# The inverse of the gated delta rule as stacked 64x64 blocks, two 64x64 tiles of the array for each product

## The chip, the cores and the metric

The kernel runs on one core of one Trainium2 chip. The metric is the time of one execution on the device, in microseconds (us); smaller is better.

## What is computed

One layer of a hybrid decoder block: 512 tokens, width 1024. A combined projection feeds sliding-window attention and a gated delta rule; their outputs are mixed, and a product-key mixture of experts (PEER) follows. The change lies in the delta rule alone: 8 heads, keys and values of 128, chunks of 64 tokens. Cut to what matters:

```python
a_low = where(strict, einsum('bhncd,bhnsd->bhncs', k_beta, kc) * decay, 0)   # 64x64 for each head and chunk
t_mat = triangular_solve(eye + a_low, eye)                                   # the inverse, 64x64
u = einsum('bhncs,bhnse->bhnce', t_mat, v_beta)
w = einsum('bhncs,bhnsd->bhncd', t_mat, k_beta * exp(gc))
qk = einsum('bhncd,bhnsd->bhncs', qc, kc) * decay
# then, one chunk after the other: v_new, o and the state
```

All of it is fp32.

## The kernel before

The program is written out phase by phase, with a queue of instructions for each engine and semaphores set by hand. The phase of the change, `phase_delta`, goes over four tiles of 128 tokens (`NT`), each of which holds two chunks of 64. Its tensors are `[128 partitions, 8 heads, 128]`; the work goes in two halves of four heads (`G = 4`, `q` = 0 or 1), one PSUM bank for each half.

In the inverse the two 64x64 matrices of a head's two chunks stand as the diagonal blocks of one 128x128 matrix, the other two blocks being zero. In a tile the order is: sums and transposes (L1019 to L1028), spreads of coefficients (L1034), the product KK of keys (L1050, banks 2 and 3), which VectorE multiplies by the masked decay `AT` that GpSimd has made (L985), and the product QK (L1058). Then come six levels of block doubling.

- Level 0: TensorE transposes AT (L1071, "P"), VectorE masks the result into `prod` (L1250) and makes `inv` and `invT` (L1291, L1292).
- Levels 1 to 5: P is the product of AT and inv (L1073, banks 0 and 1); VectorE masks it into `prod`; Q is the product of invT and prod (L1085, levels 1 to 4 alone, banks 2 and 3) and of prod and invT (L1086, banks 6 and 7); VectorE subtracts them from inv (L1298) and invT (L1300).

After the levels, u and w (L1092, L1093) use invT with 128x128 operands, and the chunk-by-chunk part follows (L1105 to L1121). TensorE takes its work in program order: P of half 0, P of half 1, Q of half 0, Q of half 1. P of a half waits for that half's invT of the level before (semaphore `D`), Q for that half's prod (`Pm`), and VectorE for `P` and `Q`.

Between these, `fill(n)` puts n passes of an independent projection (L1002, 512 columns, fp32r): 16 of them after P of level 0, and 3 after P of levels 1, 2 and 3, the last tile having none in levels 1 to 3. The number of fill passes in the phase is fixed. An fp32 product is two passes on TensorE, each with a weight load and a matmul record; a transpose is one.

Of the kernel before, what the change touches and what calls it, by code (L numbers as in the profile page):

```python
# [13 lines left out]
P = 128  # L14
KB = 1024
SEQ = 512
D = 1024
# [902 lines left out]
def phase_delta(nc, m, a, st, first_slabs):  # L920
# [6 lines left out]
    invT, q1, prod = m.at("invT", full, 72), m.at("q1", full, 76), m.at("prod", full, 76)  # L927
    AT, u = m.at("AT", full, 80), m.at("u", full, 80)
    inv, wT = m.at("inv", full, 84), m.at("wT", full, 84)
# [23 lines left out]
    with nc.Block() as block:  # L953
# [22 lines left out]
        @block.gpsimd  # L976
        def _(pool):
            nc.gpsimd.memset(S[:], 0.0).then_inc(z["prep0"], 1)
            for t in range(NT):
                if t:  # L980
                    pool.wait_ge(z["o"], t)
                for h in range(2):
                    hs = slice(G * h, G * h + G)
                    pool.wait_ge(z["E"], t * 2 + (h + 1))
                    nc.gpsimd.tensor_tensor(AT[:, hs, :], E[:, hs, :],  # L985
                                            m.strict[:].rearrange("p (o n) -> p o n", o=1).to_broadcast([P, G, P]),
                                            ALU.mult).then_inc(z["Es"], 1)

        @block.tensor
        def _(pe):  # L990
# [17 lines left out]
            def tile(t):  # L1008
# [53 lines left out]
                for l in range(6):  # L1062
                    for q in range(2):
                        if l == 0:
                            pe.wait_ge(z["AT"], t * 2 + (q + 1))
                        else:
                            pe.wait_ge(z["D"], t * 12 + (2 * l + q - 1))
                        for h in range(G * q, G * q + G):
                            o = bank[q][:, P * (h % G):P * (h % G) + P]
                            if l == 0:  # L1070
                                last = pe.transpose(o, AT[:, h, :], m.ident[:])  # L1071
                            else:
                                last = pe.matmul(o, AT[:, h, :], inv[:, h, :], start=True, stop=True)  # L1073
                        last.then_inc(z["P"], 1)
# [5 lines left out]
                    for q in range(2):  # L1080
                        pe.wait_ge(z["Pm"], t * 12 + (2 * l + q + 1))
                        for h in range(G * q, G * q + G):
                            cols = slice(P * (h % G), P * (h % G) + P)
# [12 lines left out]
                for c in range(2):  # L1096
                    rows = slice(CHUNK * c, CHUNK * c + CHUNK)
                    if c == 0:
                        pe.wait_ge(z["uwe"], t + 1)
                        if first:  # L1100
                            pe.wait_ge(z["prep0"], 1)
# [22 lines left out]
            pe.wait_ge(z["prep"], 1)  # L1124
# [75 lines left out]
        def _(dve):  # L1200
# [8 lines left out]
            v.tensor_scalar(sel[:], m.same[:], last2[:, 0:1], None, ALU.mult).then_inc(z["prep"], 1)  # L1209

            for t in range(NT):
# [35 lines left out]

                def by(q, dst, src, b, done):
# [19 lines left out]
                for q in range(2):  # L1268
                    dve.wait_ge(z["KK"], t * 2 + (q + 1))
                    dve.wait_ge(z["Es"], t * 2 + (q + 1))  # L1270
                    by(q, AT, AT[:, G * q:G * q + G, :], 2, z["AT"])
# [4 lines left out]
                eye = m.ident[:].rearrange("p (o n) -> p o n", o=1).to_broadcast([P, G, P])  # L1276
                dve.wait_ge(z["AT"], t * 2 + 2)
                for q in range(2):
                    hs = slice(G * q, G * q + G)
                    ins = v.tensor_tensor(invT[:, hs, :], AT[:, hs, :], m.above[:].rearrange("p (o n) -> p o n", o=1)  # L1280
                                          .to_broadcast([P, G, P]), ALU.mult)
                own(dve, c, ins)
                for l in range(6):
                    for q in range(2):
                        dve.wait_ge(z["P"], t * 12 + (2 * l + q + 1))
                        by(q, prod, m.level[:, l:l + 1, :].to_broadcast([P, G, P]), 0, z["Pm"])
                    if l == 0:
                        dve.wait_ge(z["Pm"], t * 12 + 2)
                        for q in range(2):
                            hs = slice(G * q, G * q + G)  # L1290
                            v.tensor_tensor(inv[:, hs, :], eye, prod[:, hs, :], ALU.subtract)  # L1291
                            v.tensor_tensor(invT[:, hs, :], eye, invT[:, hs, :], ALU.subtract).then_inc(z["D"], 1)  # L1292
# [963 lines left out]
```

## Time and profile before

| | |
|---|---|
| time, median of 3 runs | 2443.43 us (2440.55 to 2449.08) |
| span of the profiled execution | 2444.4 us |
| the delta phase in it | about 411 to 787 us |
| levels 1 to 5 of the inverse, four tiles | 119.70 us |
| TensorE busy, whole span | 2299.5 us (94%) |
| VectorE busy, whole span | 1774.4 us (73%) |

The profiled execution's own span is 1.0 us over the median of the runs, so the sum can be made against either. A level's time is read from one start of L1073 to the next. A matmul record lasts longer than the spacing to the next one, because passes overlap in the array: what a pass costs is the spacing, (length of a merged row − length of one record) / (passes − 1).

### The profile page before, as it was taken

What the parts mean: (1) busy time and instruction counts of PE and PEld (TensorE: products, weight loads), DVE (VectorE), ACT (ScalarE), POOL (GpSimd) and SP (SyncE); (2) the same over time, 40 slices, a digit from 0 to 9 for tenths busy, and PEclk for the clock granted to TensorE, in tenths of its full rate; (3) what the DMA queues carried; (4) which work ended last, traced back from release to release, by engine and by line L of the source; (5) the groups of instructions that cost most, each with busy time, mean ns of one, the idle gap of its engine ahead of it and who ended that gap; (6) DMA issues with size and microseconds to landing.
All of it is one profiled execution on the core that took longest, in us unless ns stands there. A gap on an engine that the chain in (4) does not pass through costs nothing.

```text
span 2444.4 us, 33257 instructions
## 1 busy us (share of the span) xinstructions
PE 2299.5 (94%) x12845; PEld 1989.1 (81%) x12845; DVE 1774.4 (73%) x3248; ACT 935.5 (38%) x1601; POOL 723.1 (30%) x637
## 2 busy tenths in 40 slices
PE   7898897899999999898999999899999999999998
PEld 2686776888888787678989999888888888888887
DVE  4488885554655764418978999778888888878787
ACT  2235776031131332325555555433333333333332
POOL 0444672000000000005656433533333333333330
PEclk9999997999999999899999999999999999999999
DMA  8332331010011323214333466998998889899883
GB/s 276 108 100 92 115 104 35 27 35 19 26 40 63 115 86 121 69 52 149 128 122 131 158 199 194 338 350 317 323 319 310 320 324 318 308 328 349 316 313 136
DMA packets 224989, 442.21 MB, mean 181 GB/s; under 512 B 22423, under 2 KB 138304, under 8 KB 224576
## 3 DMA queue, kind: packets, MB, share of 16 engines
q1 hardware_dynamic: 177040, 270.19, 33.0%
q0 software_dynamic: 45568, 163.60, 18.6%
q10 hardware_dynamic: 2224, 6.29, 0.6%
q8 instruction: 102, 1.67, 0.3%
q14 instruction: 55, 0.45, 0.1%
HBM read 394.16 MB, written 45.88 MB: 180 GB/s over the span
## 4 chain that ended last, share of the span: by engine, by line
PE 45%; DVE 8%; ACT 2%; issue 1%; POOL 0%; ACTq 0%; DVEq 0%
PE bank L1929 22%; PE bank L1827 5%; DVE hot_j L2145 5%; PE bank L1915 4%; PE bank L1913 4%; PE bank L1914 4%; PE bank L1833 3%; PE bank L1797 2%; DVE hot_i L2140 2%; ACT ha L1977 1%; PE bank L1807 1%; PE bank L1849 1%; DVE o_nat L2209 0%; DVE o_nat L2208 0%; PE bank L1897 0%
## 5 line engine op out<-in xcount | busy, mean ns | idle before, releaser
L1759 POOL TENSOR_TENSOR ua_lo<-ua,ua_hi 128x512 fp32r<-128x512 f32 x128 | 204.2, 1601 | 456.6 <-ACT ua L1964 456.4
L1929 PE MATMUL bank<-vt_hi,wg_hi 128*128 128x512 f32 x768 | 247.8, 404 | 5.0 <-DVE wg_lo L2199 4.8
L1752 POOL DMA_INDIRECT ug<-in_peer_u_dram,gidx x128 | 145.1, 1133 | 327.5 <-DVE ug L2155 324.5
L1929 PE MATMUL bank<-vt_lo,wg_hi 128*128 128x512 f32 x768 | 238.6, 392 | 0.0
L1929 PE MATMUL bank<-vt_hi,wg_lo 128*128 128x512 f32 x768 | 237.9, 391 | 0.0
L2181 DVE TENSOR_TENSOR vt_lo<-vt_raw,vt_hi 128x1024 fp32r<-128x1024 f32 x128 | 156.5, 1223 | 92.5 <-ACT vt_hi L2051 92.5
L1781 POOL DMA_INDIRECT vg<-in_peer_v_dram,gidx x128 | 131.5, 1027 | 238.9 <-DVE g_acc L2170 226.8
L1827 PE MATMUL bank<-h_hi,ua_hi 128*128 128x384 f32 x512 | 184.2, 360 | 12.3 <-ACT ha L1977 12.0
L1913 PE MATMUL bank<-h_hi,uT_hi 128*128 128x384 f32 x512 | 176.8, 345 | 0.0
L1827 PE MATMUL bank<-h_lo,ua_hi 128*128 128x384 f32 x512 | 173.8, 339 | 0.0
L2051 ACT ACTIVATE vt_hi<-vt_raw 128x1024 fp32r<-128x1024 f32 x128 | 135.2, 1056 | 98.7 <-PE bank L1929 98.7
L2062 ACT ACTIVATE wg_hi<-wt 128x384 fp32r<-128x384 f32 x128 | 67.3, 526 | 274.6 <-DVE wt L2194 271.4
L1915 PE MATMUL bank<-h_hi,uT_lo 128*128 128x384 f32 x512 | 171.8, 335 | 0.0
L1929 PEld LDWEIGHTS bank<-vt_hi,wg_hi 128*128 128x128 f32 x768 | 135.1, 189 | 44.9 <-issue 24.1
L1914 PE MATMUL bank<-h_lo,uT_hi 128*128 128x384 f32 x512 | 171.2, 334 | 0.0
L1929 PEld LDWEIGHTS bank<-vt_hi,wg_lo 128*128 128x128 f32 x768 | 144.5, 188 | 31.8
L1929 PEld LDWEIGHTS bank<-vt_lo,wg_hi 128*128 128x128 f32 x768 | 144.4, 188 | 31.6
L2170 DVE SCALAR_TENSOR_TENSOR g_acc<-vg,g_hw,g_acc 128x1024 f32<-128x1024 f32 x127 | 162.9, 1282 | 2.4 <-DMA vg<-in_peer_v_dram,gidx 1.3
L2155 DVE SCALAR_TENSOR_TENSOR ug<-ug,h2n 128x1024 f32<-128x1024 f32 x128 | 156.1, 1221 | 1.0 <-DMA ug<-in_peer_u_dram,gidx 0.9
L1953 ACT ACTIVATE uT_hi<-bank 128x512 fp32r<-128x512 f32 x128 | 76.0, 594 | 190.1 <-PE bank L1797 187.1
L2150 DVE TENSOR_TENSOR uT_lo<-bank,uT_hi 128x512 fp32r<-128x512 f32 x128 | 88.3, 690 | 81.9 <-ACT uT_hi L1953 81.9
L2145 DVE TENSOR_SCALAR hot_j<-iota,picked,picked 128x128 f32<-128x128 f32 x384 | 145.9, 444 | 0.0
(433 smaller groups left out, 5707.2 us busy)
## 6 DMA issues: line engine op xcount, KB each, us to landing
u_raw<-in_peer_u_dram SPq DMA_DIRECT2D x128, 512.0 KB
vt_raw<-in_peer_v_dram SPq DMA_DIRECT2D x128, 512.0 KB
gates<-g_stage SPq DMA_DIRECT2D x12, 2048.0 KB, 9.0
gate<-gates SPq DMA_DIRECT2D x32, 768.0 KB, 7.6
pj_raw<-in_w_in_dram SPq DMA_DIRECT2D x16, 1024.0 KB, 5.2
ada_w<-in_w_ada_dram POOLq DMA_DIRECT2D x32, 512.0 KB, 4.6
hid_keep<-ha POOLq DMA_DIRECT2D x64, 192.0 KB
hl<-hid_keep SPq DMA_DIRECT2D x64, 192.0 KB
```

The costliest lines, as they stand in the source:

```text
L1752: nc.gpsimd.indirect_dma_start(ug[s % RING][:], None, u_rows, bass.IndirectOffsetOnAxis(m.gidx[:, s:s + 1].bitcast(U32), 0)).then_inc(s_ug ...
L1759: nc.gpsimd.tensor_tensor(ua_lo[b % 2][:, 4 * q:4 * q + 4, :], ua[b % 2][:, 4 * q:4 * q + 4, :], ua_hi[b % 2][:, 4 * q:4 * q + 4, :].bitca ...
L1827: last = pe.matmul(o, ua_hi[b % 2][:, k, :], (m.h2_lo if low else m.h2_hi)[:, k, P:], start=(n == 0), stop=False)
L1913: pe.matmul(o, uT_hi[f % 2][:, k, :], m.h2_hi[:, k, P:], start=(k == 0), stop=False)
L1914: pe.matmul(o, uT_hi[f % 2][:, k, :], m.h2_lo[:, k, P:], start=False, stop=False)
L1915: last = pe.matmul(o, uT_lo[f % 2][:, k, :], m.h2_hi[:, k, P:], start=False, stop=(k == KC - 1))
L1929: ins = pe.matmul(y_bank[t][q][:], w[n % 2][:, tok], v[n % 2][:, 512 * q:512 * q + 512], start=(first and i == 0), stop=(last and i == 2))
L2051: nc.scalar.activation(v_hi[n % 2][:], v_raw[n % 4][:], ACT.Copy).then_inc(x["vhi"], 1)
L2145: ins = v.tensor_scalar(B[n % 4][:, t, :], m.iota[:], jT[:, col], gT[:, col], ALU.is_equal, ALU.mult)
L2155: v.scalar_tensor_tensor(ug[s % RING][:], ug[s % RING][:], 1.0, m.h2n[:], ALU.mult, ALU.mult, accum_out=h_raw[:, s:s + 1]).then_inc(x["dot ...
L2170: ins = v.scalar_tensor_tensor(acc[:], vg[s % RING][:], h_w[:, s:s + 1], acc[:], ALU.mult, ALU.add)
L2181: v.tensor_tensor(v_lo[n % 2][:], v_raw[n % 4][:], v_hi[n % 2][:].bitcast(F32), ALU.subtract)\
```

## The change

The two 64x64 blocks of a head are no longer kept as a 128x128 matrix with two zero blocks, but stacked: chunk 0 on partitions 0 to 63, chunk 1 on partitions 64 to 127, 64 columns a head. Each 128x128 product of the inverse becomes two 64x64 products, `for rows in CH`: one reads partitions 0 to 63 and writes partitions 0 to 63 of the bank, the other reads 64 to 127 and writes 64 to 127. VectorE's operations over the inverse have 256 elements a partition in place of 512. The first level's transposes become products with a stacked identity `eye`. The last level writes the result back into the two diagonal blocks of the 128x128 `invT`, whose other blocks were zeroed once. KK is computed for the two diagonal blocks alone, and GpSimd masks them with two operations of 64 partitions. The core of the diff:

```diff
+    pair = [P, DNH, CHUNK]
+    prod, AT = m.at("prod", pair, 76), m.at("AT", pair, 80)
+    inv, tinv = m.at("inv", pair, 84), m.at("tinv", pair, 86)
+    eye, near = m.at("eye", [P, CHUNK], 96), m.at("near", [P, CHUNK], 96.25)
+    step = m.at("step", [P, 6, CHUNK], 96.5)
+    CH = [slice(CHUNK * c, CHUNK * c + CHUNK) for c in range(2)]
...
+            nc.gpsimd.memset(invT[:], 0.0).then_inc(z["prep0"], 1)
+            pool.wait_ge(z["prep0"], 2)
...
-                    nc.gpsimd.tensor_tensor(AT[:, hs, :], E[:, hs, :],
-                                            m.strict[:].rearrange("p (o n) -> p o n", o=1).to_broadcast([P, G, P]),
-                                            ALU.mult).then_inc(z["Es"], 1)
+                    if t * 2 + h:
+                        pool.wait_ge(z["Es"], t * 4 + 2 * h)
+                    for c, rows in enumerate(CH):
+                        if c:
+                            pool.wait_ge(z["Es"], t * 4 + 2 * h + 1)
+                        nc.gpsimd.tensor_tensor(AT[rows, hs, :], E[rows, hs, rows],
+                                                m.strict[rows, rows].rearrange("p (o n) -> p o n", o=1)
+                                                .to_broadcast([CHUNK, G, CHUNK]), ALU.mult).then_inc(z["Es"], 1)
...
-                    last = pe.matmul(bank[2 + h // G][:, P * (h % G):P * (h % G) + P], kT[:, h, :], kb[:, h, :],
-                                     start=True, stop=True)
+                    cols = slice(CHUNK * (h % G), CHUNK * (h % G) + CHUNK)
+                    for rows in CH:
+                        last = pe.matmul(bank[2 + h // G][rows, cols], kT[:, h, rows], kb[:, h, rows],
+                                         start=True, stop=True)
...
-                            o = bank[q][:, P * (h % G):P * (h % G) + P]
-                            if l == 0:
-                                last = pe.transpose(o, AT[:, h, :], m.ident[:])
-                            else:
-                                last = pe.matmul(o, AT[:, h, :], inv[:, h, :], start=True, stop=True)
+                            cols = slice(CHUNK * (h % G), CHUNK * (h % G) + CHUNK)
+                            for rows in CH:
+                                last = pe.matmul(bank[q][rows, cols], AT[rows, h, :],
+                                                 inv[rows, h, :] if l else eye[rows, :], start=True, stop=True)
...
                             if l < 5:
-                                pe.matmul(bank[2 + q][:, cols], invT[:, h, :], prod[:, h, :], start=True, stop=True)
-                            last = pe.matmul(bank[6 + q][:, cols], prod[:, h, :], invT[:, h, :], start=True, stop=True)
+                                for rows in CH:
+                                    pe.matmul(bank[2 + q][rows, cols], tinv[rows, h, :], prod[rows, h, :],
+                                              start=True, stop=True)
+                            for rows in CH:
+                                last = pe.matmul(bank[6 + q][rows, cols], prod[rows, h, :], tinv[rows, h, :],
+                                                 start=True, stop=True)
...
+            v.tensor_tensor(eye[:], m.ident[:, CH[0]], m.ident[:, CH[1]], ALU.add).then_inc(z["prep"], 1)
+            v.tensor_tensor(near[:], m.above[:, CH[0]], m.above[:, CH[1]], ALU.add)
+            own(dve, c, v.tensor_tensor(step[:], m.level[:, :, CH[0]], m.level[:, :, CH[1]], ALU.add))
...
+                def stacked(b):
+                    return bank[b][:, 0:G * CHUNK].rearrange("p (h n) -> p h n", h=G)
...
-                            v.tensor_tensor(inv[:, hs, :], inv[:, hs, :],
-                                            bank[2 + q][:].rearrange("p (h n) -> p h n", h=G), ALU.subtract)
-                        v.tensor_tensor(invT[:, hs, :], invT[:, hs, :],
-                                        bank[6 + q][:].rearrange("p (h n) -> p h n", h=G), ALU.subtract)\
-                            .then_inc(z["D"], 1)
+                            v.tensor_tensor(inv[:, hs, :], inv[:, hs, :], stacked(2 + q), ALU.subtract)
+                            ins = v.tensor_tensor(tinv[:, hs, :], tinv[:, hs, :], stacked(6 + q), ALU.subtract)
+                        else:
+                            dve.wait_ge(z["prep0"], 2)
+                            for rows in CH:
+                                ins = v.tensor_tensor(invT[rows, hs, rows], tinv[rows, hs, :],
+                                                      bank[6 + q][rows, 0:G * CHUNK].rearrange("p (h n) -> p h n", h=G),
+                                                      ALU.subtract)
+                        ins.then_inc(z["D"], 1)
```

## Rows read from the trace of the kernel before

**Rows 1.** The page: engines over the span, and the granted clock in 40 slices
```profile
PE 2299.5 (94%) x12845; PEld 1989.1 (81%) x12845; DVE 1774.4 (73%) x3248; ACT 935.5 (38%) x1601; POOL 723.1 (30%) x637
...
PEclk9999997999999999899999999999999999999999
```

**Rows 2.** Windows: levels 1 to 5 of tiles 0 to 3
```profile
core 0: us, PE busy (x) PEld busy (x) DVE busy (x) ACT busy (x) POOL busy (x), PEclk, DMA share, GB/s
458.80:489.36 30.56, 28.62 (x234) 27.23 (x234) 18.55 (x29) 0.00 (x0) 0.00 (x0) 1.00 0.01 1
550.48:580.73 30.25, 28.31 (x235) 27.07 (x233) 17.91 (x28) 0.00 (x0) 0.00 (x0) 1.00 0.00 1
643.01:673.59 30.58, 28.64 (x234) 27.23 (x234) 18.55 (x29) 0.00 (x0) 0.00 (x0) 1.00 0.00 1
734.67:762.98 28.31, 26.37 (x225) 25.45 (x224) 17.95 (x28) 0.84 (x1) 0.00 (x0) 1.00 0.03 10
```

**Rows 3.** Timeline of TensorE, level 3 of the last tile (no fill)
```profile
start us, us, engine line op out<-in xcount [idle before <-releaser]
...
752.40 1.06 PE L1073 MATMUL bank<-inv,AT 128*128 128x128 f32 x8
753.94 1.16 PE L1073 MATMUL bank<-inv,AT 128*128 128x128 f32 x8 [0.48 <-DVE invT L1300]
754.93 0.39 PE L1085 MATMUL bank<-prod,invT 128*128 128x128 f32 x2
...
758.51 0.28 PE L1073 MATMUL bank<-inv,AT 128*128 128x128 f32 x1
```

**Rows 4.** Timeline of TensorE, level 2 of tile 1 (with fill)
```profile
556.53 1.06 PE L1073 MATMUL bank<-inv,AT 128*128 128x128 f32 x8
...
559.30 0.40 PE L1002 MATMUL bank<-h_hi,fl_hi 128*128 128x512 f32 x1
559.53 0.40 PE L1002 MATMUL bank<-h_lo,fl_hi 128*128 128x512 f32 x1
...
563.34 0.39 PE L1073 MATMUL bank<-inv,AT 128*128 128x128 f32 x2
```

**Rows 5.** Timeline of TensorE: attention, 64-column and 64-row operands in turn
```profile
248.10 1.15 PE L638 MATMUL bank<-pT,av 128*64 128x128 f32 x16
249.17 1.14 PE L608 MATMUL bank<-kn,aq 64*128 64x256 f32 x8
```

**Rows 6.** Timeline of TensorE: delta phase, 64-column operands on one side alone
```profile
768.88 1.96 PE L1105 MATMUL bank<-states,wT 128*64 128x128 f32 x16 [0.31 <-ACT wT L1188]
770.76 2.00 PE L1110 MATMUL bank<-qg,states 128*128 128x64 f32 x16
...
773.59 0.39 PE L1002 MATMUL bank<-h_lo,fl_hi 128*128 128x512 f32 x1
773.82 0.40 PE L1002 MATMUL bank<-h_hi,fl_lo 128*128 128x512 f32 x1
774.14 1.04 PE L1115 MATMUL bank<-vnew,kdec 64*128 64x128 f32 x7
```

**Rows 7.** Groups by form: VectorE's 512- and 256-element operations
```profile
L1250 DVE TENSOR_TENSOR prod<-level,bank 128x512 f32<-128x512 f32 x48 | 32.6, 685 | 13.4 <-PE bank L1073 13.1
L798 DVE SCALAR_TENSOR_TENSOR sc<-bank,qrs,amask 128x256 f32<-128x256 f32 x64 | 26.4, 475 | 0.2 <-PE bank L608 0.2
L819 DVE COPY aq<-bank 128x256 f32<-128x256 f32 x16 | 6.4, 403 | 0.0
```

**Rows 8.** Groups by form: GpSimd's products
```profile
L985 POOL TENSOR_TENSOR AT<-E,strict 128x512 f32<-128x512 f32 x8 | 13.8, 1730 | 303.8 <-DVE E L1264 303.8
L528 POOL TENSOR_TENSOR ada_w<-ada_w 128x256 f32<-128x256 f32 x32 | 31.6, 988 | 2.5
```

**Rows 9.** Timelines of TensorE and VectorE: level 0, last tile and tile 2
```profile
727.61 0.66 PE L1071 MATMUL bank<-ident,AT 128*128 128x128 f32 x4 [2.67 <-DVE AT L1250]
728.93 1.01 PE L1071 MATMUL bank<-ident,AT 128*128 128x128 f32 x4 [0.67 <-DVE AT L1250]
...
731.01 0.63 PE L1002 MATMUL bank<-h_hi,fl_hi 128*128 128x512 f32 x1
731.44 0.63 PE L1002 MATMUL bank<-h_lo,fl_hi 128*128 128x512 f32 x1
...
643.01 0.68 PE L1073 MATMUL bank<-inv,AT 128*128 128x128 f32 x4 [0.81 <-DVE invT L1292]
```

More of the change, by code:

```diff
@@ L926, in phase_delta @@
     E = m.at("E", full, 68)
-    invT, q1, prod = m.at("invT", full, 72), m.at("q1", full, 76), m.at("prod", full, 76)
-    AT, u = m.at("AT", full, 80), m.at("u", full, 80)
-    inv, wT = m.at("inv", full, 84), m.at("wT", full, 84)
+    pair = [P, DNH, CHUNK]
+    invT, q1 = m.at("invT", full, 72), m.at("q1", full, 76)
+    prod, AT = m.at("prod", pair, 76), m.at("AT", pair, 80)
+    inv, tinv = m.at("inv", pair, 84), m.at("tinv", pair, 86)
+    u, wT = m.at("u", full, 80), m.at("wT", full, 84)
+    eye, near = m.at("eye", [P, CHUNK], 96), m.at("near", [P, CHUNK], 96.25)
+    step = m.at("step", [P, 6, CHUNK], 96.5)
+    CH = [slice(CHUNK * c, CHUNK * c + CHUNK) for c in range(2)]
     sq = m.at("dn_sq", [P, 2 * DNH, P], 76)
@@ L1082, in tile @@
                         for h in range(G * q, G * q + G):
-                            cols = slice(P * (h % G), P * (h % G) + P)
+                            cols = slice(CHUNK * (h % G), CHUNK * (h % G) + CHUNK)
                             if l < 5:
-                                pe.matmul(bank[2 + q][:, cols], invT[:, h, :], prod[:, h, :], start=True, stop=True)
-                            last = pe.matmul(bank[6 + q][:, cols], prod[:, h, :], invT[:, h, :], start=True, stop=True)
+                                for rows in CH:
[4 more added lines that the diff above has]
+                                                 start=True, stop=True)
                         last.then_inc(z["Q"], 1)
@@ L1100, in tile @@
                         if first:
-                            pe.wait_ge(z["prep0"], 1)
+                            pe.wait_ge(z["prep0"], 2)
                     else:
@@ L1123, in tile @@
                 last.then_inc(z["o"], 1)
-            pe.wait_ge(z["prep"], 1)
+            pe.wait_ge(z["prep"], 2)
             for t in range(NT):
@@ L1269, in _ @@
                     dve.wait_ge(z["KK"], t * 2 + (q + 1))
-                    dve.wait_ge(z["Es"], t * 2 + (q + 1))
-                    by(q, AT, AT[:, G * q:G * q + G, :], 2, z["AT"])
+                    dve.wait_ge(z["Es"], t * 4 + 2 * q + 2)
+                    hs = slice(G * q, G * q + G)
+                    v.tensor_tensor(AT[:, hs, :], AT[:, hs, :], stacked(2 + q), ALU.mult).then_inc(z["AT"], 1)
                 for q in range(2):
@@ L1275, in _ @@
                     by(q, E, E[:, G * q:G * q + G, :], 6, z["QKT"])
-                eye = m.ident[:].rearrange("p (o n) -> p o n", o=1).to_broadcast([P, G, P])
+                unit = eye[:].rearrange("p (o n) -> p o n", o=1).to_broadcast([P, G, CHUNK])
                 dve.wait_ge(z["AT"], t * 2 + 2)
@@ L1279, in _ @@
                     hs = slice(G * q, G * q + G)
-                    ins = v.tensor_tensor(invT[:, hs, :], AT[:, hs, :], m.above[:].rearrange("p (o n) -> p o n", o=1)
-                                          .to_broadcast([P, G, P]), ALU.mult)
+                    ins = v.tensor_tensor(tinv[:, hs, :], AT[:, hs, :], near[:].rearrange("p (o n) -> p o n", o=1)
+                                          .to_broadcast([P, G, CHUNK]), ALU.mult)
                 own(dve, c, ins)
@@ L1285, in _ @@
                         dve.wait_ge(z["P"], t * 12 + (2 * l + q + 1))
-                        by(q, prod, m.level[:, l:l + 1, :].to_broadcast([P, G, P]), 0, z["Pm"])
+                        v.tensor_tensor(prod[:, G * q:G * q + G, :], step[:, l:l + 1, :].to_broadcast([P, G, CHUNK]),
+                                        stacked(q), ALU.mult).then_inc(z["Pm"], 1)
                     if l == 0:
@@ L1290, in _ @@
                             hs = slice(G * q, G * q + G)
-                            v.tensor_tensor(inv[:, hs, :], eye, prod[:, hs, :], ALU.subtract)
-                            v.tensor_tensor(invT[:, hs, :], eye, invT[:, hs, :], ALU.subtract).then_inc(z["D"], 1)
+                            v.tensor_tensor(inv[:, hs, :], unit, prod[:, hs, :], ALU.subtract)
+                            v.tensor_tensor(tinv[:, hs, :], unit, tinv[:, hs, :], ALU.subtract).then_inc(z["D"], 1)
                         continue
```

## The prediction

> **What bounds the kernel now.** I read the page first: TensorE is busy 94% of the span and VectorE 73%, and the granted clock is full nearly everywhere [rows 1]. That is an average over phases, so I cut out the stretches the change touches: levels 1 to 5 of the four tiles last 30.56, 30.25, 30.58 and 28.31 us, together 119.70 us or 4.9% of the span, with TensorE busy 93% of each at full clock and VectorE about 60% [rows 2]. Nothing outside the delta phase is touched, and the phases follow each other, so what the inverse saves comes off the end nearly whole.
>
> Then one level. In the last tile, which has no fill there, P of one level starts at 752.40 and P of the next at 758.51, so a level is 6.11 us [rows 3]. It is 48 passes: 8 + 8 for P, 16 + 16 for Q. The first row gives a pass: (1.06 − 0.28) / 7 = 0.112 us, so 48 × 0.112 = 5.38 us. The rest, 0.73 us, is mainly the wait of the second half's P for VectorE's invT (0.48). With three fill passes of 0.23 us a level is 6.81 us, 556.53 to 563.34 [rows 4]. So TensorE's stream of passes sets the level, and VectorE's six operations of 0.685 us [rows 7] mostly hide under it.
>
> **The price of a 64x64 pass.** A head's product is two fp32 passes now and four small ones afterwards, so the change pays if a small pass costs under half of 0.112 us. No row shows a pass with 64 rows, 64 weight columns and 64 moving columns. The nearest:
>
> - Halving one side alone gives nothing: 64 weight columns with 128 moving ones cost (1.96 − 0.28) / 15 = 0.112 us, 128 weight columns with 64 moving ones (2.00 − 0.28) / 15 = 0.115 [rows 6]. The longer of the two sides sets the pace. With both at 64 a single stream should come to half, about 0.055.
> - Two tiles at once give another half. In attention, L638 uses 64 weight columns and changes between the two column halves: 16 passes in 1.15 us, (1.15 − 0.27) / 15 = 0.059 each, where L1105 with the same shape in one half pays 0.112. L608 changes between the two row halves: (1.14 − 0.38) / 7 = 0.109 for 256 moving columns, where 128 cost 0.112 in one stream [rows 5, 6].
>
> Both together make a quarter of 0.112, or 0.028, and half of 0.059, or 0.030. I take 0.030. Ends: 0.0275 below, and above a full 0.112 (nothing gained from either).
>
> The Trainium skill ("TensorE: Matmul & The Clock Gate", "Back-to-back issue gap") has a rule against the change: with hardware decode off the sequencer spends about 62 ns on a matmul, and small ones go no faster. L638's 0.059 lies just under it, but in a burst of 16 alone, so the trace barely speaks against it. By 62 ns a level's 96 passes would be 5.95 us, and by 0.030 they are 2.88.
>
> **Levels, part by part.** VectorE: 512 elements take 0.685 us and start 0.60 apart; 256 fewer elements, at the rate that 0.403 to 0.475 us for 256 from PSUM confirms [rows 7], make about 0.42 us, 0.34 apart. Six of them are 2.1 us a level, still under TensorE.
>
> A changed level without fill:
> - 96 passes × 0.030 = 2.88 us;
> - a wait: after the last pass of Q has started, it lands (0.22), VectorE does inv and tinv (0.34 + 0.42) and the signals take 0.09: 1.07 us, of which P of the first half covers 16 × 0.030 = 0.48. That leaves 0.57.
>
> Sum 3.45 us for 6.11. With fill there come 3 × 0.23 = 0.69, and two changes between full and small tiles. At such a change the gap is wider: L1105's last start, 768.88 + 1.96 − 0.28 = 770.56, to 770.76 is 0.20 for 0.11 and the row's first pass adds 0.05; 773.82 to 774.14 is 0.32 for 0.23 and the first pass adds 0.1 [rows 6]. So 0.14 to 0.19 each, and I take 0.16. Sum 4.46 us for 6.81. Level 1 begins with both halves ready and so costs 4.2 and 3.2. Level 5 has only 64 passes (1.92), the wait, and a tail of two operations of 64 partitions in place of one, 3.1 us in all.
>
> Per tile with fill: 4.2 + 4.46 + 4.46 + 3.45 + 3.1 = 19.7 us; last tile: 3.2 + 3 × 3.45 + 3.1 = 16.7. Against [rows 2]: (30.56 + 30.25 + 30.58) − 3 × 19.7 = 32.3, and 28.31 − 16.7 = 11.6. **Levels: −43.9 us.**
>
> **Level 0 and KK.** The eight transposes (one pass each) become 32 small passes, 0.96 us for 0.9, plus changes of tile size on both sides of them and before level 1. The 16 fill passes stay. Where TensorE comes late (the last tile) this costs 0.1 us a tile. Where it waits for VectorE, 0.85 us in tile 0 and 0.81 in tile 2 [rows 9], VectorE's shorter operations end the wait, which gives 0.7 each. Together **−1.2 us**. KK (16 passes to 32 small ones) gains up to 0.8 us on TensorE, which I cost at nothing: behind it TensorE waits 2.67 us for AT anyway [rows 9]. If that cover were gone it would be a gain.
>
> GpSimd's two masks per half: 128x512 took 1.73 us in the mean, a 256-element product elsewhere 0.99 [rows 8]. Two in a row are 1.3 (half price) to 3.5 us (full price), and I take 2.0. AT is then up to 0.3 us later, which VectorE's shorter AT operation (−0.26) pays back. At full price 4 × 1.7 = 7 us would be lost; behind the second mask in its queue is nothing but the next tile's. The memset, `eye`, `near` and `step` lie under ACT's squares at the phase's start: nothing, at most 1 us. No DMA changes.
>
> **The clock.** In level 0 of the last tile the fill passes stand 0.43 apart instead of 0.23 (731.01, 731.44) [rows 9]: half clock, after 2.67 us of waiting. The shorter KK lengthens that wait, and the levels leave the array emptier. One more such stretch in a tile, 8 slow passes × 0.2, costs 1.6 us. I put in **+3 us** for four tiles (between 0 and 6.4).
>
> **Sum:** 2443.4 − 43.9 − 1.2 + 3 = 2401.3; I say **2402 us**, −1.7%.
>
> **Rivals.**
> 1. *Two tiles do not run at once.* L638's two halves share a bank but read all rows; L608's two row halves write two banks. The changed products read different rows and write one bank, which no row shows. If they take turns, a pass costs 0.0545: 5.23 us a level, with the wait about 5.4 (fill 6.4), level 5 3.9; per tile 28.4 and 25.3. Saved: 91.4 − 85.2 + 28.3 − 25.3 = 9 us, so 2436 us (2434 to 2441 with clock and level 0). For it: nothing in the rows. The Trainium skill says it outright ("TensorEngine Tiling (Array Packing)", "Gotcha 1: PSUM Pressure"): different row tiles cannot use one PSUM bank simultaneously. No run here shows it.
> 2. *The stream of instructions is the bound.* Each small pass still has its weight load and its matmul, so a level has 192 instructions for 96. If no pass goes below L638's 0.059, a level is 5.7 (fill 6.7) and the time is 2440 to 2444 us: no change. The skill's 62 ns would give the same.
> 3. *The clock falls in the levels.* Passes at 0.055 and fill at 0.43: 2441 us; half of the stretch so, 2421. Against it: full clock in all of [rows 2], whose waits are under 0.5 us.
> 4. *Slower.* The array drains at every change of tile, which happens after every two passes. Then a pair pays part of the 0.16 us, and 0.055 + 0.04 a pass makes 9.1 us a level. Level time goes over today's once a pass passes about 0.060. At 0.095 the loss is 3 us × 16 levels + 4 × 2 = 56 us: 2500 us. At the bound of 0.112 it is about 100 us. L638 and L608, which change tile every four passes, speak against it.
> 5. *The pace is good but something else takes part back* (VectorE as the bound, GpSimd's masks at full price, late fill): passes of 0.04 or 10 us lost elsewhere, 2414.
>
> **Chances.** Forecast (2393 to 2408) 0.60, rival 5 0.15, rival 1 0.10, rival 2 0.05, rival 3 0.04, rival 4 0.06. What a measurement tells from no change is 0.3%, 7.3 us: faster is under 2436. Faster: 0.60 + 0.15, half of rival 1 (0.05) and of rival 3 (0.02), 0.82; within it: the rest of rivals 1, 2 and 3, 0.12; slower 0.06. Range 2390 to 2434: forecast, rival 5 and a part of 1 and 3; its upper end stands for passes of 0.054. The forecast's own is 2393 (0.0275 and no clock loss) to 2408.
>
> **What would show it.** In the timeline P starts of L1073's successor 3.4 to 3.5 us apart in the last tile and 4.4 to 4.6 with fill; 16 passes of P in 0.7 us; the windows of levels 1 to 5 at about 76 us in sum; clock 1.00 in them; VectorE's operations 0.42 us; GpSimd's masks 0.8 to 1.1. A merged row of 16 passes that lasts 1.1 us means rival 1 or 2: starts in pairs tell 1 from 2. It would be wrong if small passes stand 0.055 or more apart.

## The result, and the profile after

Over four executions each the changed kernel takes 2410.61 us (2405.57 to 2412.26) and the kernel before 2445.63 us (2440.55 to 2449.08): ratio 0.9848, interval 0.9830 to 0.9867. The forecast was 2402 us, so the sign is right and 35 of the 41 us came. The profiled execution of the changed kernel has a span of 2410.4 us for 2444.4. One execution among all the runs below, 3206.55 us at a granted clock of 0.65 throughout, is in no median.

The windows of levels 1 to 5, tiles 0 to 3, in the changed kernel (against [rows 2]; columns as there), and below them the whole delta phase:

```profile
core 0: us, PE busy (x) PEld busy (x) DVE busy (x) ACT busy (x) POOL busy (x), PEclk, DMA share, GB/s
461.79:481.08 19.29, 18.01 (x459) 15.53 (x458) 10.73 (x29) 0.00 (x0) 0.00 (x0) 1.00 0.01 3
544.23:563.54 19.31, 18.03 (x459) 15.53 (x458) 10.74 (x29) 0.00 (x0) 0.00 (x0) 1.00 0.02 4
626.63:645.93 19.30, 18.02 (x459) 15.53 (x458) 10.74 (x29) 0.00 (x0) 0.00 (x0) 1.00 0.04 12
708.86:725.31 16.45, 15.12 (x449) 13.92 (x448) 10.73 (x29) 0.75 (x1) 0.00 (x0) 1.00 0.05 19
412.62:749.72 337.10, 313.74 (x3506) 278.23 (x3507) 160.10 (x417) 79.42 (x154) 15.42 (x16) 0.91 0.13 37
```

The four levels' windows sum to 74.35 us for 119.70, at full clock and with twice the records. The last row is the news: the whole phase has a mean granted clock of 0.91. (The window ends just after the last tile's product o has begun; that product takes 2.05 us in both kernels.) The same window of the kernel before reads 0.95:

```profile
411.60:785.90 374.30, 348.40 (x2450) 318.73 (x2451) 197.01 (x409) 79.32 (x154) 13.84 (x8) 0.95 0.11 33
```

So the phase went from 374.30 to 337.10 us, 37.2 less, where the levels alone gave 45.35. Laid out by stage (from the first matmul of each to that of the next, sum of four tiles, us; fill counts to the stage that it follows; gcn and cf are the two sets of coefficients that the spreads copy over the columns; states and o are the chunk-by-chunk part):

| stage | before | after | difference |
|---|---|---|---|
| squares, transposes | 34.72 | 36.93 | +2.2 |
| spreads of gcn | 32.31 | 33.42 | +1.1 |
| spreads of cf | 21.49 | 21.80 | +0.3 |
| KK | 9.94 | 7.80 | -2.1 |
| QK and the wait for AT | 15.70 | 16.32 | +0.6 |
| level 0 | 27.08 | 31.37 | **+4.3** |
| levels 1 to 5 | 119.70 | 74.35 | **-45.35** |
| u and w | 23.81 | 24.20 | +0.4 |
| states | 67.25 | 68.64 | +1.4 |
| o | 22.29 | 22.27 | 0 |

One level with fill, in TensorE's timeline of the changed kernel (tile 1, against [rows 4]):

```profile
start us, us, engine line op out<-in xcount [idle before <-releaser]
...
548.20 0.68 PE L1085 MATMUL bank<-inv,AT 64*64 64x64 f32 x16
549.13 0.68 PE L1085 MATMUL bank<-inv,AT 64*64 64x64 f32 x16 [0.25 <-DVE tinv L1324]
...
550.33 0.40 PE L1014 MATMUL bank<-h_lo,fl_hi 128*128 128x512 f32 x1
550.65 0.33 PE L1099 MATMUL bank<-prod,tinv 64*64 64x64 f32 x4
550.82 0.28 PE L1102 MATMUL bank<-tinv,prod 64*64 64x64 f32 x4
550.93 0.28 PE L1099 MATMUL bank<-prod,tinv 64*64 64x64 f32 x4
...
552.65 0.56 PE L1085 MATMUL bank<-inv,AT 64*64 64x64 f32 x11
```

P starts at 548.20 and again at 552.65, 4.45 us. Sixteen passes of P last 0.68, so (0.68 - 0.22) / 15 = 0.031 us each; from the second on, Q's groups of four start 0.117 apart (550.82, 550.93), 0.029 a pass. The wait for `tinv` is 0.25. From 550.33 to 550.65, fill to small tile, is 0.32 for 0.23. In the last tile P starts at 715.47 and 718.87, 3.40 us.

And level 0 of the last tile (against [rows 9]):

```profile
701.40 0.68 PE L1085 MATMUL bank<-eye,AT 64*64 64x64 f32 x16 [2.53 <-DVE AT L1295]
702.97 1.12 PE L1085 MATMUL bank<-eye,AT 64*64 64x64 f32 x16 [0.89 <-DVE AT L1295]
...
704.62 0.63 PE L1014 MATMUL bank<-h_lo,fl_hi 128*128 128x512 f32 x1
705.04 0.63 PE L1014 MATMUL bank<-h_hi,fl_lo 128*128 128x512 f32 x1
```

A wait of 2.53 us, one of 0.89, and then fill passes start 0.43 apart (704.62, 705.04), the clock's lower level of 1.2 GHz, until from 706.28 on they are back at 0.23. The changed kernel has this in every tile, after waits for AT of 1.96, 1.97, 1.97 and 2.53 us; in tile 0 the slow passes go from 455.74 to 460.17, ten gaps. The record of the granted clock has 61 us at the lower level within the phase, and 41 before.

In the kernel before the waits were 1.72, 1.75, 1.75 and 2.67 us, and the clock fell in tile 1 and the last alone. Tiles 1 and 2 had the same waits; the length of the second row (1.09 for 0.66) shows the clock:

```profile
543.38 0.66 PE L1071 MATMUL bank<-ident,AT 128*128 128x128 f32 x4 [1.75 <-DVE AT L1250]
544.71 1.09 PE L1071 MATMUL bank<-ident,AT 128*128 128x128 f32 x4 [0.66 <-DVE AT L1250]
...
636.55 0.66 PE L1071 MATMUL bank<-ident,AT 128*128 128x128 f32 x4 [1.75 <-DVE AT L1250]
637.87 0.66 PE L1071 MATMUL bank<-ident,AT 128*128 128x128 f32 x4 [0.67 <-DVE AT L1250]
```

So the length of the wait alone does not decide. What ends the two waits is seen in VectorE's timeline of tile 0, changed kernel:

```profile
451.52 1.21 DVE L1223 TENSOR_TENSOR fl_lo<-fl_raw,fl_hi 128x1024 fp32r<-128x1024 f32 x1
452.65 0.41 DVE L1295 TENSOR_TENSOR AT<-AT,bank 128x256 f32<-128x256 f32 x1
454.21 0.42 DVE L1295 TENSOR_TENSOR AT<-AT,bank 128x256 f32<-128x256 f32 x1 [1.15 <-POOL AT L997]
```

The first half's AT comes when VectorE gets to it in its own queue, the second half's when GpSimd has done its masks (L997).

The rest of the kernel took 3.2 us more (1.0 ahead of the phase, 2.2 behind it), where no instruction differs. Profiles differ by as much: among the thirteen of this study the phase begins between 405.6 and 413.5 us, and what follows it takes 1656.6 us in the kernel before and 1657.4 to 1661.2 in the others. Whether the 2.2 us behind it are chance is not shown.

### The profile page after: what moved, and what is told of

It reads as the page before. It is cut to its first block, busy times and chain, and to the rows that moved or that the text cites. A ratio compares the mean times of both kernels' runs of the same rounds, so it can differ in the third digit from the quotient of the medians.

```text
span 2410.4 us, 35403 instructions
## 1 busy us (share of the span) xinstructions
PE 2266.5 (94%) x13901; PEld 1949.0 (81%) x13901; DVE 1738.7 (72%) x3259; ACT 935.9 (39%) x1601; POOL 721.0 (30%) x646
## 4 chain that ended last, share of the span: by engine, by line
PE 45%; DVE 8%; ACT 2%; issue 1%; DMA 0%; POOL 0%; ACTq 0%; DVEq 0%; POOLq 0%
PE bank L1958 22%; PE bank L1856 5%; DVE hot_j L2174 5%; PE bank L1944 4%; PE bank L1942 4%; PE bank L1943 4%; PE bank L1862 3%; PE bank L1826 2%; DVE hot_i L2169 2%; PE bank L1836 1%; ACT ha L2006 1%; PE bank L1878 1%; DMA vg<-in_peer_v_dram,gidx 0%; DVE o_nat L2238 0%; DVE o_nat L2237 0%
## 5 line engine op out<-in xcount | busy, mean ns | idle before, releaser
L1781 POOL DMA_INDIRECT ug<-in_peer_u_dram,gidx x128 | 144.3, 1127 | 330.4 <-DVE ug L2184 327.3
```

The costliest lines, as they stand in the source:

```text
L1781: nc.gpsimd.indirect_dma_start(ug[s % RING][:], None, u_rows, bass.IndirectOffsetOnAxis(m.gidx[:, s:s + 1].bitcast(U32), 0)).then_inc(s_ug ...
```

## The experiments

The questions: what makes the levels short (theory A: two tiles at once, not the smaller shape), how much of it needs VectorE's shorter operations, and where the 8 us between the levels' gain and the phase's went (theory C: the clock, lowered by the wait for AT). There are eleven runs, of which one is the changed kernel again and one repeats another run. Where no interval is given the time is that of a single execution, and the reading rests on its profile. In the code, "..." stands for the rest of a line, or for lines between.

### Both products on one tile

```diff
-                            for rows in CH:
+                            for rows in ((CH[0], CH[0], CH[1]) if l else CH):
                                 last = pe.matmul(bank[q][rows, cols], AT[rows, h, :], ...
```

In levels 1 to 5 chunk 0's products are computed twice on their own tile, and chunk 1's once. Q has the same edit.

> In levels 1 to 5 the product of chunk 0 is computed twice, both times on tile rows 0-63 / columns 0-63; the product of chunk 1 once. A level has 144 small passes in place of 96, 96 of them on one tile. Theory A (a tile takes 0.055 us a pass and the two tiles run at once): the tile with 96 passes sets the level, 96 x 0.0545 = 5.2 us and a wait, so a level without fill is 5.4 to 5.8 us in place of 3.40, and a half's P of 24 passes lasts about 0.95 us from first to last start. Theory B (all passes go through one point that takes 0.029 us each): 144 x 0.029 = 4.2 us and a wait, so a level of 4.5 to 4.8 us and 0.67 us for a half's P.

Time 2450.32 us. The window of levels 1 to 5 in the last tile (it was 16.45 us), and the start of level 1's Q in TensorE's timeline:

```profile
736.06:762.97 26.91, 26.89 (x673) 26.49 (x672) 11.06 (x28) 0.73 (x1) 0.00 (x0) 1.00 0.04 13
```
```profile
737.97 0.39 PE L1099 MATMUL bank<-prod,tinv 64*64 64x64 f32 x6
738.21 0.39 PE L1102 MATMUL bank<-tinv,prod 64*64 64x64 f32 x6
```

Six passes, four on tile 0 and two on tile 1, every 0.233 us: that is 4 x 0.058, tile 0's passes one after the other, with tile 1's hidden beside them. The change has four passes there, in 0.117: half as many passes again double the price. A level without fill is 5.74 us (P from 741.71 to 747.44), inside theory A's range and not B's 4.5 to 4.8. A 64x64 pass costs 0.058 on its tile, and only the second tile makes 0.029 of it. The levels sum to 116.93 us, nearly the 119.70 of before.

### A third tile beside the two

```diff
+                            if l:
+                                pe.matmul(bank[2 + q][CH[1], over], AT[CH[0], h, :], inv[CH[0], h, :], start=True, stop=True)
                             for rows in CH:
                                 last = pe.matmul(bank[q][rows, cols], AT[rows, h, :], ...
```

The same number of extra products, but on the tile that reads rows 0 to 63 and writes partitions 64 to 127 (Q alike); their results are not used.

> As many passes as in the kernel with chunk 0 doubled (144 a level), but the extra product runs on a third tile (rows 0-63, columns 64-127) and its result goes to a part of a bank that nobody reads. Theory A (tiles are independent, issue is fast): the third tile costs nothing, level without fill 3.4 to 3.6 us. Theory B (one point, 0.029 us a pass): 4.5 to 4.8 us, the same as with the extra product on the same tile.

Time 2414.8 us. TensorE's timeline in P of the last tile: L1086 is the extra product, L1088 the two of the change:

```profile
714.75 0.22 PE L1088 MATMUL bank<-inv,AT 64*64 64x64 f32 x2
714.76 0.22 PE L1086 MATMUL bank<-inv,AT 64*64 64x64 f32 x1
714.80 0.22 PE L1088 MATMUL bank<-inv,AT 64*64 64x64 f32 x2
```

Three passes now start in the 0.05 to 0.06 us in which two did. The levels sum to 79.08 us for 74.35: 50% more passes for 6% more time. Most of that 6% is in one row of the groups, levels 1 to 5 of tile 1:

```profile
L1088 PE MATMUL bank<-inv,AT 64*64 64x64 f32 x160 | 6.7, 224 | 0.9 <-issue 0.9
```

0.9 of the 1.1 us by which this tile is longer is idle time that no wait explains, in the middle of a row: in its last level 16 passes of P have started by 560.1, and the 17th starts at 561.21. So the supply of instructions (rival 2) may begin to show at three tiles; at the two of the change it is the single tile's 0.058 that binds.

### Chunk 0 first, then chunk 1

```diff
-                        for h in range(G * q, G * q + G):
-                            for rows in CH:
+                        for rows in CH:
+                            for h in range(G * q, G * q + G):
```

The same products in another order within a half: 8 passes of P, or 16 of Q, on one tile before the other's.

> The same products in another order: in each half first all of chunk 0 (one tile), then all of chunk 1 (the other tile), so the tile changes every 8 or 16 passes and not every 2. If the array starts a tile's pass as soon as that tile is free, looking at least 8 to 16 passes ahead: level unchanged, 3.4 to 3.6 us without fill. If it looks ahead only a few passes, the two tiles run one after the other: 0.055 a pass, a half's P of 16 passes 0.85 us and a level of 5.4 to 5.8 us.

Time 2442.99 us, nearly that of the kernel before. The levels sum to 100.64 us, 19 under those of before, but level 0 takes 35.33 and 68 us of the phase are at the lower clock. TensorE's timeline where Q's last half meets the next level's P (L1099, L1101: Q of chunk 1; L1085: P of chunk 0):

```profile
740.54 0.28 PE L1099 MATMUL bank<-prod,tinv 64*64 64x64 f32 x2
...
740.77 0.22 PE L1099 MATMUL bank<-prod,tinv 64*64 64x64 f32 x1
740.78 0.27 PE L1085 MATMUL bank<-inv,AT 64*64 64x64 f32 x1
...
740.95 0.22 PE L1085 MATMUL bank<-inv,AT 64*64 64x64 f32 x1
740.95 0.22 PE L1101 MATMUL bank<-tinv,prod 64*64 64x64 f32 x1
741.00 0.74 PE L1085 MATMUL bank<-inv,AT 64*64 64x64 f32 x13
```

Up to 740.77 the four passes from 740.54 on, all on one tile, take 0.23: 0.058 each. At the change of tile the next tile's passes begin while the last four of the old one (740.77 to 740.95) are still starting: pairs for 0.23 us, then single file again. So TensorE looks only a few passes ahead, which is what the rows allow; what limits it inside, no run tells. The order `for h: for rows` of the change is what earns 26.3 (100.64 - 74.35) of the levels' 45 us.

### The tile changed every four passes

```diff
                         for h in range(G * q, G * q + G):
-                            if l < 5:
-                                for rows in CH:
-                                    pe.matmul(bank[2 + q][rows, cols], tinv[rows, h, :], ...
-                            for rows in CH:
-                                last = pe.matmul(bank[6 + q][rows, cols], prod[rows, h, :], ...
+                            for rows in CH:
+                                if l < 5:
+                                    pe.matmul(bank[2 + q][rows, cols], tinv[rows, h, :], ...
+                                last = pe.matmul(bank[6 + q][rows, cols], prod[rows, h, :], ...
```

P takes the heads in twos, in the same way.

> The same products, but the tile changes after four passes and not after two (P takes two heads of chunk 0, then two of chunk 1; Q both products of a head's chunk 0, then both of chunk 1). The run with chunk 0's products all first had 16 passes of P in 0.96 us for 0.68, so a change of tile hid about 0.1 us, two passes of 0.055. Theory J (each change hides about that much, which is all of two passes and half of four, in both directions): passes at 0.028 to 0.035 still, a level without fill 3.4 to 3.8 us, levels 1 to 5 of the four tiles 74 to 80 us. Rival K (only neighbours that belong to different tiles overlap, one pair for each change): passes at 0.042 or more, a level of 4.3 us or more, 90 us or more in sum.

Time 2415.72 us; the levels sum to 75.54 us, 1.2 more than the change has. In TensorE's timeline of the last tile a level is 721.69 - 718.25 = 3.44 us:

```profile
718.25 0.73 PE L1086 MATMUL bank<-inv,AT 64*64 64x64 f32 x16
...
721.69 0.73 PE L1086 MATMUL bank<-inv,AT 64*64 64x64 f32 x16
```

Theory J holds: four passes on one tile, then four on the other, still pair almost fully. The look-ahead spans four passes and not eight (P of the run before has eight on a tile, and its half took 0.96 us for 0.68).

### VectorE's operations doubled

```diff
+                        if l:
+                            v.tensor_tensor(spare[q][:], step[:, l:l + 1, :].to_broadcast([P, G, CHUNK]), stacked(q), ALU.mult)
                         v.tensor_tensor(prod[:, G * q:G * q + G, :], step[:, l:l + 1, :].to_broadcast([P, G, CHUNK]),
                                         stacked(q), ALU.mult).then_inc(z["Pm"], 1)
```

So for each of the six operations of levels 1 to 4 and the prods of level 5; the copies' results are not used.

> Each of VectorE's operations in levels 1 to 5 has a copy before it whose result nobody reads, so VectorE has about the load of before and TensorE the passes of the change. It tells how much of the gain needed VectorE's shorter operations. Theory G (TensorE's passes alone set the level): 3.40 us a level stays within 0.3 us. Rival H (with passes at 0.030 the two engines are near to each other, so VectorE at 2 x 0.34 an operation becomes the bound): a level without fill is 4.1 to 4.8 us (6 x 0.68 = 4.1 and a wait), with fill about 4.9, and levels 1 to 5 sum to 85 to 98 us for 74.4: about 2425 us.

Time 2434.73 us, the levels 93.48 us in sum. TensorE's timeline of the last tile:

```profile
729.77 0.68 PE L1086 MATMUL bank<-inv,AT 64*64 64x64 f32 x16 [0.58 <-DVE tinv L1329]
731.10 0.68 PE L1086 MATMUL bank<-inv,AT 64*64 64x64 f32 x16 [0.64 <-DVE tinv L1329]
...
734.42 0.68 PE L1086 MATMUL bank<-inv,AT 64*64 64x64 f32 x16 [0.58 <-DVE tinv L1329]
```

A level is 4.65 us for 3.40; the waits for `tinv` are 0.58 and 0.64. Twelve operations start 0.33 apart, 4.0 us: VectorE sets the level. Rival H holds. The load is somewhat above that of before (six operations 0.60 apart, 3.6 us), so the run is a bound: TensorE's shorter passes alone give at least 119.70 - 93.48 = 26.2 of the 45.35 us, and at most 19.1 needed the halved operands of VectorE.

### QK computed twice: the clock behind the wait for AT

```diff
                 for h in range(DNH):
+                    pe.matmul(bank[6 + h // G][:, P * (h % G):P * (h % G) + P], kT[:, h, :], q1[:, h, :],
+                              start=True, stop=True)
                     last = pe.matmul(bank[6 + h // G][:, P * (h % G):P * (h % G) + P], kT[:, h, :], q1[:, h, :],
                                      start=True, stop=True)
```

1.8 us of useless work in each tile, put in the wait for AT.

> The product QK, whose end is followed by a wait of 1.97 to 2.53 us for AT, is computed twice: 16 more passes of 0.112 us, 1.8 us more work in each of the four tiles. Theory C (level 0 is longer than before because the clock falls to half after that wait): the half-clock stretches at level 0 go, P of level 0 to P of level 1 becomes about 6.0 us a tile in place of 7.5 to 8.7, and the time falls by 4 to 8 us against the changed kernel, to 2403 to 2407. Rival D (level 0's length is not the clock's doing): time the same or up to 1 us longer, 2410 to 2412.

2403.15 us (four executions, 2394.93 to 2409.76), ratio 0.9818, interval 0.9776 to 0.9860. The median is 7 us under the change's; the two intervals overlap, so the times alone do not show it. The profile does: with more work in it the phase is 7.1 us shorter, 5.6 of them in level 0 (25.77 us in sum for 31.37). The windows of level 0 in this run, tile 0 and the last (tiles 1 and 2 are 6.04 and 6.03):

```profile
453.42:459.48 6.06, 5.16 (x49) 4.01 (x49) 4.47 (x11) 1.55 (x2) 0.92 (x2) 1.00 0.32 88
...
694.40:702.03 7.63, 6.73 (x49) 5.17 (x49) 4.48 (x11) 0.83 (x2) 0.92 (x2) 0.78 0.01 2
```

and of the same tiles in the changed kernel:

```profile
453.12:461.79 8.67, 7.83 (x49) 6.03 (x49) 4.47 (x11) 1.54 (x2) 0.91 (x2) 0.61 0.22 61
...
701.40:708.86 7.46, 6.57 (x48) 5.17 (x48) 4.47 (x11) 0.79 (x2) 0.92 (x2) 0.77 0.00 0
```

The instructions are the same; the clock column makes the difference, 6.04 us at 1.00 against 7.5 to 8.7 at 0.61 to 0.78. In the last tile, which has no fill ahead of QK, a wait of 0.74 us is left and the clock falls still. Theory C holds for level 0. The squares, transposes and gcn spreads keep 68.7 us of the change's 70.35 (67.03 before), so about half of what they lost is still lost with the wait filled in three tiles.

### The fill put in the wait

```diff
+                fill(8)
                 for l in range(6):
...
-                        fill(16 if l == 0 else 0 if last_tile else 3)
+                        fill(8 if l == 0 else 0 if last_tile else 3)
```

Useful work in place of useless: eight of level 0's sixteen fill passes stand between QK and the wait for AT. The changed kernel itself went along on the same chip, as the yardstick.

> The changed kernel itself, as the yardstick for the two runs that move fill. Every theory: 2405 to 2413 us, ratio 0.983 to 0.987; level 0 of the four tiles 31 us, levels 1 to 5 74.4 us, fill passes 0.43 apart in every tile's level 0.

> Eight of level 0's sixteen fill passes stand ahead of the wait for AT; same work, other order. Theory C (the 2 to 2.5 us of waiting for AT lower the clock and the fill behind it pays): the eight passes (8 x 0.23 = 1.84 us) take up the wait, the passes stay 0.23 apart, and level 0 is then bound by VectorE's chain, about 5.0 us a tile (AT at 536.6, inv and tinv of half 0 at 541.5 in the changed kernel), so level 0 sums to 20 to 22 us for 31.4, and the time is about 2400 us. Rival D (the stretch at half clock comes whatever TensorE does, or moves on into the levels): level 0 loses only the eight passes that left it, about 24 us in sum, a half-clock stretch is still there in each tile or lies in level 1, and the time is 2404 or more.

The changed kernel: 2411.06 us (2399.82 to 2412.53), ratio 0.9842, interval 0.9819 to 0.9865, level 0 31.35 us in sum. With the fill moved: 2392.69 us (2389.67 to 2396.82), ratio 0.9780, interval 0.9760 to 0.9799. The window of level 0 in the last tile:

```profile
682.88:687.99 5.11, 3.40 (x41) 2.54 (x41) 3.95 (x10) 1.54 (x2) 0.91 (x2) 1.00 0.04 17
```

Level 0 sums to 20.48 us, the stage ahead of it stays at 16.36, and the clock is full: theory C holds, and the 5.1 us a tile are VectorE's chain, with 1.15 us of waiting for GpSimd's masks in it. In the last tile waits of 0.70 and 0.89 us are left and the clock stays up, where after 0.74 and 0.90 it fell in the run with QK twice. The phase, up to the last tile's o, takes 327.3 us for 337.1; that o then takes 3.78 for 2.05, at the lower clock. Seven more microseconds in the profile came from ahead of the phase, where the code is the same, so the kernel ran once more:

> The run with eight fill passes ahead of the wait for AT once more. In the profile of the first the delta phase began 7.0 us earlier than in the changed kernel's, from less time at half clock before it, where the code is the same. If that was chance, it begins at about 412 us here, level 0 is 20.5 us in sum again, and the time is 2393 to 2402 us. If it is a property of this kernel, it begins at about 405 again and the time is 2390 to 2396.

2402.63 us (2392.55 to 2405.34), ratio 0.9805, interval 0.9781 to 0.9829. The phase begins at 413.5 and takes 326.9 us, level 0 20.46. The median is just above the 2393 to 2402 expected. So the seven are no property of this kernel, though what makes them no run tells; the 10.9 us of level 0 repeat. The same kernel has medians 10 us apart in the two runs, on different chips: a difference of that size between runs of different chips has to be looked for in the stages.

### The fill out of the levels, and between the halves

```diff
-                        fill(16 if l == 0 else 0 if last_tile else 3)
+                        fill((17 if not last_tile else 8) if l == 0 else 0 if last_tile else 0)
```

on top of `fill(8)` ahead of the wait.

> As the run before, and the nine fill passes of levels 1 to 3 are moved to level 0 (17 there in tiles 0 to 2, 8 in the last). Theory E (a level with fill costs 4.44 us for 3.40 because of 3 x 0.23 of fill and 0.35 of changes between tile sizes): levels 1 to 5 of tiles 0 to 2 fall from 19.3 to 16.2 us, 65 us in sum for 74.4; level 0 is about 6.3 us in tiles 0 to 2 and 5 to 5.5 in the last, 24.4 in sum; the time is about 2394 us. Rival F (with no fill among them the levels have too little work on TensorE and the clock falls in them): the levels stay at 19 us or more in sum over a tile at a clock under 1.00, and the time is 2405 or more.

2395.63 us over five executions (2385.32 to 2397.51), ratio 0.9784, interval 0.9761 to 0.9807. The windows of levels 1 to 5, and of level 0, in tile 1:

```profile
536.17:552.61 16.44, 15.11 (x449) 13.91 (x448) 10.73 (x29) 0.00 (x0) 0.00 (x0) 1.00 0.02 4
529.88:536.17 6.29, 5.39 (x50) 4.20 (x50) 4.47 (x11) 1.45 (x2) 0.93 (x2) 1.00 0.31 83
```

The levels fall to 65.80 us, level 0 is 23.99, and the clock stays at 1.00 in levels without fill; rival F falls. The phase takes 319.9 us. In the time, this run can't be told from the two with the fill moved (2392.69 and 2402.63): the intervals overlap with both.

The last edit puts three of level 0's passes where TensorE still waits 0.90 us for the second half's AT:

```diff
                         last.then_inc(z["P"], 1)
+                        if l == 0 and q == 0:
+                            fill(3)
```

with 14 passes behind (5 in the last tile).

> As the run with fill taken out of the levels, and three of level 0's fill passes stand between the halves of P, where TensorE waits 0.90 us for AT of the second half. Three passes (0.69) and two changes of tile size (0.3) fill the wait, so level 0 has three passes less behind it: 6.3 - 0.7 = 5.6 us in tiles 0 to 2 if TensorE still bounds it, and 5.1 in the last, which VectorE bounds. Level 0 22 us in sum for 24.0, nothing else moves, and the time is 2 us under that run, 2392 to 2396; against the changed kernel -15 to -19 us. Rival: the second half of P comes later than AT (by up to 0.15 us) and VectorE's chain with it, then level 0 stays at 24 us.

2385.36 us (2381.99 to 2393.82), ratio 0.9748, interval 0.9726 to 0.9770. TensorE's timeline of tile 1: no wait is left in level 0.

```profile
526.61 0.68 PE L1086 MATMUL bank<-eye,AT 64*64 64x64 f32 x16
527.22 0.50 PE L1014 MATMUL bank<-h_hi,fl_hi 128*128 128x512 f32 x1
...
528.20 0.68 PE L1086 MATMUL bank<-eye,AT 64*64 64x64 f32 x16
```

Level 0 sums to 21.91 us as expected. The phase takes 320.8 us (up to the last o), no less than in the run before, because the states of the last tile took 23.2 us for 20.0, with 24 us in a row at the lower clock there for 7; the median is below the 2392 to 2396 expected, by more than the 2 us that level 0 explains, and what the rest is stays open. It is the lowest median of the study, 25 us under the change; its interval overlaps that of the run before, so that these three passes gain time is shown in level 0 alone.

## Why the prediction was right, and where it was off

- **Levels 1 to 5, right: -45.35 us for -43.9.** A pass is 0.029 to 0.031 for the 0.030 taken; a level is 3.40 (3.45) and with fill 4.45 (4.46). The windows are 19.3 for 19.7 and 16.45 for 16.7.
- **Halving both sides, then two tiles, right.** The product of the two guesses (half for the shape, half for the pairing) is what the runs show apart: 0.112 to 0.058 on one tile, and to 0.029 with two. What the prediction did not see is that the second half hangs on the order: with a change of tile after 8 and 16 passes the levels are 100.6 us.
- **VectorE "still under TensorE", right by little.** Its operations take 0.42 us and start 0.34 apart, as worked out. With a load somewhat above that of before it was the bound (93.5 us in the levels).
- **Rival 1, no.** Two tiles that read different rows and write different partitions of one PSUM bank do run at once: four passes in one bank take 0.117 us, where four on one tile take 0.233. The Trainium skill ("TensorEngine Tiling (Array Packing)", "Gotcha 1: PSUM Pressure") says that different row tiles cannot use one bank simultaneously; the trace disagrees, with 0.117 us for four passes, two on each row tile, that write different partitions of one bank.
- **Rival 2, no.** 144 passes a level took 6% longer than 96; passes stand 0.029 us apart with two tiles and under 0.020 with three. The Trainium skill ("TensorE: Matmul & The Clock Gate", "Back-to-back issue gap") gives about 62 ns a matmul for hardware decode switched off; no run tells how it is set here, and these distances show that no such bound holds.
- **Rival 3, no.** The granted clock is 1.00 in all four windows of the levels.
- **Rival 4, no.** A change of small tile every two passes costs nothing; the two changes between full and small tile in a level with fill cost 4.45 - 3.40 - 0.69 = 0.36 us for the 0.32 taken.
- **KK at nothing, right.** It is 2.1 us shorter on TensorE, but AT does not hang on it: the end of the wait moves only with VectorE's own queue. From the spreads of cf to level 0 the four tiles lose 47.13 - 45.92 = 1.2 us, which is VectorE's AT operation (0.41 us for 0.68) four times. GpSimd's two masks of a half are 2 x 0.964 = 1.9 us for the 2.0 taken, and the second half's AT follows the first by 1.56 us for 1.31: 0.25 later, as the prediction allowed.
- **The step that failed in size: the clock.** "Together -1.2 us" for level 0 and KK and "+3 us for four tiles" for the clock make +1.8; the stages beside the levels gave +8.1. The first term came out better than forecast: at full clock level 0 takes 6.04 us a tile where it took 6.46 (tiles 0 and 2 of before), -1.7, and with the -1.2 ahead of it -2.9. The clock is the term that was too small. In level 0 it costs 31.37 - 4 x 6.04 = 7.2 us in the changed kernel and cost 27.08 - 4 x 6.46 = 1.2 before, so +6.0 there alone (an estimate, as it takes 6.04 and 6.46 for all four tiles). The runs with the wait filled bear it out: level 0 is 6.04 us there in three tiles with useless work, and 5.1 in all four with fill passes. Another +4.7 stand in squares, gcn and states, whose instructions did not change; that they are the clock's is read from its record and not tested. The prediction had the mechanism (half clock behind the wait for AT) and its price, 1.6 us a tile or 6.4 in all, and then took half of it, "+3", without a reason, and nothing for the stages around level 0.
- **The forecast's own range, missed.** 2410.6 us lies outside the 2393 to 2408 that went with 2402, and nearer to rival 5's 2414 ("the pace is good but something else takes part back"). Rival 5 named VectorE, GpSimd's masks and late fill for it; what took it back was the clock.
- **Outside the phase** 3.2 us, for which the prediction had nothing and no run has a cause.

The sum again, in the profiled spans: -45.35 for -43.9, +8.1 for +1.8, +3.2 for 0: -34.0 for -42.1. That the levels gave 1.5 us more than forecast hides as much of the clock's cost.

## What to carry to other kernels

Splitting block-diagonal fp32 products into 64x64 tiles gained next to nothing in time here until neighbours in the stream went to different tiles: look at the price of one tile first (0.058 us), then at the order. When TensorE's work shrinks, price the waits that it used to cover, and look at what stands right behind them: here the passes behind the waits lost 7.2 us to the clock, and eight of them put into the wait took level 0 from 31.4 to 20.5 us. And where the levels alternate between two engines, halve both sides: with VectorE's load left high, up to 19 of the 45 us would have been lost.

## What the runs showed of the hardware

- A third 64x64 tile beside two is nearly free: 79.08 us for 74.35 with 144 passes a level in place of 96.
- TensorE overlaps passes of two tiles only over a short stretch of its stream: almost fully with four passes on a tile (75.54 us for 74.35), for the last four of 16 only (740.77 to 740.95).
- In all four tiles of the changed kernel a wait of 1.96 to 2.53 us and one of 0.84 to 0.89 were followed by a stretch at 1.2 GHz, which fell on the dense work behind them. Shorter waits came out both ways: 1.75 and 0.66 with it in tile 1 of the kernel before and without it in tile 2; 0.74 and 0.90 with it (QK twice, last tile), 0.70 and 0.89 without it (fill moved, last tile).
